# The loads of combine's residual rows, moved behind the last expert's weights

## The reference, cut to what matters

```python
x = x + g1 * (merged @ w_out)
h2 = rms_norm(x) * (1.0 + sc2) + sh2
x = x + g2 * hier_moe(h2, w_rg, b_rg, w_re, b_re, w_gate, w_up, w_down)
```

## Time and profile before

| | |
|---|---|
| median of 3 runs | 1881.39 us (1880.12 to 1888.14) |
| profiled execution, its own time | 1881.47 us |
| its span in the profile | 1879.6 us |
| PE busy | 1624.2 us, 86% of the span |
| DVE busy | 850.9 us, 45% |
| ACT busy | 350.0 us, 19% |
| POOL busy | 222.8 us, 12% |
| moved by DMA | 197.16 MB, mean 105 GB/s |

### The profile page before, as it was taken

How to read it: one execution, slowest core, us unless ns; L and a number is a source line. 1 busy time by engine, 2 the same in 40 slices (tenths; PEclk the granted TensorE clock), 3 DMA queues, 4 the chain that set the end, 5 groups by cost and what they waited for, 6 DMA issues and landing times. The chain is left out here.

```text
span 1879.6 us, 18009 instructions
## 1 busy us (share of the span) xinstructions
PE 1624.2 (86%) x6099; PEld 955.6 (51%) x6100; DVE 850.9 (45%) x1740; ACT 350.0 (19%) x726; POOL 222.8 (12%) x387
## 2 busy tenths in 40 slices
PE   7799968869879799999989999899997299899980
PEld 1455623367734466666646777654554244444440
DVE  1311219855057999999983333332111511111116
ACT  2311110011145111111114444400111011111110
POOL 0000020000031011111110000000322012222220
PEclk9899989967589899999999999899998599999995
DMA  9100035420010311122100300052222846667647
GB/s 341 63 4 4 5 107 186 131 27 3 1 32 12 115 58 58 58 59 78 60 30 0 138 1 1 21 198 74 101 97 78 300 148 216 239 218 274 218 157 285
DMA packets 139193, 197.16 MB, mean 105 GB/s; under 512 B 30741, under 2 KB 106069, under 8 KB 138789
## 3 DMA queue, kind: packets, MB, share of 16 engines
q1 hardware_dynamic: 125714, 156.69, 25.5%
q0 software_dynamic: 8800, 28.52, 4.1%
q10 hardware_dynamic: 4612, 11.05, 1.7%
HBM read 154.94 MB, written 39.17 MB: 103 GB/s over the span
## 5 line engine op out<-in xcount | busy, mean ns | idle before, releaser
L1153 DVE TENSOR_SCALAR_CACHE_REDUCE tk_hits<-sc,tk_cand 128x384 bf16<-128x384 f32 (+6 forms) x217 | 250.5, 1154 | 7.7
L1119 PE MATMUL ps<-hT,gt_w 128*128 128x352 f32 (+1 forms) x768 | 240.6, 472 | 12.8 <-DMA gt_w<-in_w_glu 12.8
L1909 PE MATMUL ps<-ex_wgu,ex_xT 128*128 x416 | 187.0, 603 | 17.8 <-SPq L1824 12.1
L1119 PEld LDWEIGHTS ps<-hT,gt_w 128*128 128x128 f32 x768 | 147.1, 192 | 102.5 <-DMA gt_w<-in_w_glu 13.4
L1909 PEld LDWEIGHTS ps<-ex_wgu,ex_xT 128*128 128x128 f32 x416 | 78.1, 193 | 110.0 <-issue 110.0
L1500 PE MATMUL ps<-hT,mergedT 128*128 128x512 f32 (+1 forms) x288 | 127.6, 602 | 4.7 <-DMA op_wr<-in_w_route_expert 4.7
L1119 PE MATMUL ps<-zT,gt_w 128*128 128x352 f32 (+1 forms) x384 | 120.9, 468 | 0.0
L1331 DVE CUSTOM_DVE_ANT_0 at_s<-ps,mask 128x1024 f32<-128x1024 f32 (+8 forms) x76 | 58.8, 778 | 104.1 <-PE ps L1243 91.4
L1982 DVE SCALAR_TENSOR_TENSOR ex_hid<-ex_silu,ex_weight,ps 128x256 f32<-128x256 f32 x26 | 12.5, 480 | 202.0 <-ACT ex_silu L1954 202.0
L1119 PEld LDWEIGHTS ps<-zT,gt_w 128*128 128x128 f32 x384 | 73.0, 190 | 44.0
L1930 PE MATMUL ps<-ex_wd,ex_hidT 128*128 x208 | 93.6, 592 | 0.2 <-DVE ex_hidT L1989 0.2
(11 more groups left out here) (428 smaller groups left out, 2156.6 us busy)
## 6 DMA issues: line engine op xcount, KB each, us to landing
ex_wgu<-in_w_gate SPq DMA_DIRECT2D x16, 1024.0 KB, 5.9
ex_wgu<-in_w_up SPq DMA_DIRECT2D x16, 1024.0 KB, 11.0
ex_wd<-in_w_down SPq DMA_DIRECT2D x16, 1024.0 KB, 12.9
sp_ada_w<-in_w_ada SPq DMA_DIRECT2D x14, 1024.0 KB
gt_w<-in_w_in SPq DMA_DIRECT2D x16, 512.0 KB, 5.3
cb_y<-y_dram ACTq DMA_DIRECT2D x16, 512.0 KB, 8.3
merge_left_dram<-qiT SPq DMA_DIRECT2D x8, 544.0 KB, 6.3
mg_gb<-gate_b_dram SPq DMA_DIRECT2D x8, 544.0 KB, 3.7
```

What stands on the lines that cost most here:

```text
L1119: i = nc.tensor.matmul(m.ps[:, seq % 8, 0:n], w[:, c % NB, at + k, :], rhs[:, k, lo:lo + n], start=k == 0, stop=k == nk - 1)
L1153: return v.tensor_scalar(hits[0:r, 0:w], m.sc[0:r, c:c + w], scalar, 0.0, ALU.is_ge, ALU.add, accum_out=cnt[0:r, j:j + 1])
L1909: j = nc.tensor.matmul(m.ps[:, 2 + b, :], xT[:, b, k, :], wgu[:, bass.ds(at, 1), k, :].rearrange("p o n -> p (o n)"), start=k == 0, stop=k ...
```

## The change

The loop that issues the nine loads of the residual rows is moved on SP: from between `weights_here(0)` and the loop over the experts 3 to 15 to behind that loop, ahead of the last two calls of `weights_here`. The loads themselves, their places and their semaphore are the same, and so is every other instruction.

```diff
--- before.py
+++ after.py
@@ -1824,13 +1824,13 @@
                     sp.sem_inc(here, 1)
 
                 weights_here(0)
-                for t in range(TILES):
-                    sp.dma_start(m.x1[t][0:rows_of(t), :], m.x1_dram[t * P:t * P + rows_of(t), :]).then_inc(m.x1l, 16)
                 for e in range(RING, NE):
                     weights_here(e - RING + 1)
                     used = sp.value_load(m.expert_done[0:1, e - RING:e - RING + 1], min_val=1, max_val=MAXT)
                     sp.wait_ge(dn, used)
                     load_expert(nc, sp, m, A, e)
+                for t in range(TILES):
+                    sp.dma_start(m.x1[t][0:rows_of(t), :], m.x1_dram[t * P:t * P + rows_of(t), :]).then_inc(m.x1l, 16)
                 for e in range(NE - RING + 1, NE):
                     weights_here(e)
```

## The result

The changed kernel took 1891.35 us (median of 12 runs, 1886.93 to 1899.81) beside 1881.6 us for the kernel before in the same comparison: a ratio of 1.005, 95% interval 1.0033 to 1.0066, which is 9.4 us, between 6.2 and 12.4. A later comparison with runs of its own gave 1890.89 beside 1885.08: 1.0027 (1.0009 to 1.0045), 5.1 us. The change makes the kernel slower by about 0.4%, some 7 us; the forecast was +4.7 us. One run of a kernel further down (the signals first) took 2064.89 us, in a slower state of the chip, and is left out of that kernel's figures. The profiled execution took 1893.06 us, its span 1891.2.

A forecast was written before the change was run, and what follows sets the result against it. PE's matmul tiles bound the expert stage, through waits for first gathers (12.5 us) and SP's weight signals (12.1 us). Terms -4.6 (gathers) + 7.4 (late signal) + 1.9 (clock) = +4.7 on 1881.47 gave 1886.2 us, range 1881.5 to 1891.0.

The forecast's parts named there:

- the rows' transfer was hidden: Before combine: residual rows leave the queue by 1812.7, PE's last matmul ends at 1827.70, so 15 us are left.
- no hold: Rival at SP's late issues: an issue counts as done once its own packets are listed; +1.7 us, 1883.2 us, chance 0.2.
- By bytes: Rival at SP's queue: megabytes, not packets, fill it; signal 14.2 us late, +11.5, 1892.9 us, chance 0.12.
- PE is not held by it: Rival: PE's idle before 1789.39 had another, earlier cause, so only the gain is left; 1876.8 us, chance 0.05.
- the size of the hold: At the nine late issues on SP: the signal comes 7.4 us later than 1789.0, bounds 4.4 to 8.9.
- that gate load: The third expert's gate load on SP, ended with 1598 packets left; taken as the room for the nine issues.
- the one bound: Room of 1331 packets, from the second expert's up load: SP free at 1797.9, signal 8.9 us late.
- The gain: At the first two gathers, with the nine loads gone: second transposes start 4.6 us earlier, bounds 3.4 and 4.9.
- empty-queue price of 4.4 us: Landing time of a gather with SP's queue empty, applied to both first gathers to get the 4.6 us.
- The clock: At PE's late idle: the granted clock falls and costs 1.9 us, bounds 1.7 and 2.0.
- no measurable change: Whole kernel: the forecast lies within half a per cent, 9.4 us; chance of staying within 0.84.
- the range: Whole kernel's predicted time: 1881.5 to 1891.0 us.

The follow-up runs named there:

- the signals first: Against the kernel before, SP signals expert e-1 ahead of issuing expert e's loads: row loads in the new place 1873.97 us (0.9936), in the old place 1877.18 us (0.9952).
- the second profile: The changed kernel unedited, timed and profiled again beside the kernel before: ratio 1.0027 (1.0009 to 1.0045).
- the loads behind the signal: Against the changed kernel, the nine row loads stand behind the signal for expert 14, ahead of expert 15's: 1882.23 us, 0.9996 of the kernel before.
- no loads at all: Against the changed kernel, the nine row loads and combine's wait for them are left out: 1881.29 us, 0.999 of the kernel before.
- the rows loaded twice: Against the changed kernel, all nine row loads are also issued at the old place, combine waiting for eighteen: 1895.19 us, 1.0064 of the kernel before.
- two loads ahead: Against the changed kernel, two of the nine row loads stay ahead of the signal for expert 14, seven go behind it: one run, 1883.6 us.

## Why the prediction went as it did

**The mechanism, step by step, was right.** The gathers gained, the nine issues were held by the last expert's packets, the signal behind them came late, PE waited for it and met the low clock, the rows' transfer was hidden. Of the rivals, *no hold* doesn't agree with the runs: a load of 64 rows held SP for 6.58 us and one of 1024 rows for 0.60. The Trainium skill, page "Perfetto Trace Analysis", section "DMA Instruction — HWDGE (DVE, Sync)", behind that rival, has the sequencer free when its own instruction's descriptors have been generated; these two times differ from it, and the measurement decides. *By bytes* doesn't fit either: when the ninth issue ended, 7.34 - 2.43 = 4.9 MB were outstanding, where 3.15 would have been its limit. *PE is not held by it* falls with the 10.75 us.

**The step that failed is the size of the hold.** "I take 7.4, because eight of the nine stand behind a load of few packets, as that gate load did": the hold came to 8.70 us. The room (the packets of earlier loads still outstanding when an issue ends) was not 1598 packets but 1342 at the ninth issue's end, close to the 1331 that had been taken as the one bound (its 8.9 us hit). The row chosen as nearest ended its issue after 0.71 us, so it may not have been held to its limit at all. The prediction had a nearer one, the row load that the first stage's weights held for 5.72 us, which ended with 1310 left; it was used against *by bytes* alone. But the kernel before had no single room to read: its other three issues that were held long, the second expert's down load and the third's up and down loads, ended at 1467.09, 1471.40 and 1475.55, when this many packets of SP's queue from 1455 were through:

```profile
q1 hardware_dynamic: 3138, 3.67, 91.9%
...
q1 hardware_dynamic: 4617, 5.17, 96.4%
...
q1 hardware_dynamic: 5446, 6.77, 98.1%
```

4720, 6032 and 7072 packets stood ahead of them, so 1582, 1415 and 1626 were left. What sets the room between 1310 and 1626 no run shows.

**The gain was a little over-sized.** 4.6 was forecast, 3.77 measured. The single empty-queue price of 4.4 us held for the first gather (4.5), but the second, issued 1.84 us behind it, took 5.5; the bound of 3.4 us, from a gather of 5.8, was nearer.

**The clock** was sized at 1.9 and cost 2.05 us (1.5 in the second profile, 8.64 - 7.13).

**What can be told from no change** was put at half a per cent. The first comparison's interval reaches 0.17% to either side, so a change of 0.5% is clear of noise there; the forecast's "no measurable change" was too coarse.

Together the measured terms give -3.77 + 8.70 + 2.05 = +7.0 us instead of +4.7. The two comparisons, +9.4 (6.2 to 12.4) and +5.1 (1.7 to 8.5), both contain it, and their mean is 7.2. On the median of before shown at first the terms make 1888.4; the measured median lies 3 us above that, and 0.35 us above the range's upper end of 1891.0. That remainder is not a part of the change that the runs could find: before itself had medians of 1881.6, 1883.78, 1884.27 and 1885.08 us in four comparisons, which is as wide. The second comparison's 1890.89 us lie within the range; on which side of its end a median falls is chance at this size, the 2.3 us between +4.7 and +7.0 are not.

What stays open is how much of the 3.8 us at the first gathers reaches the end. Against before, the loads behind the signal and no loads at all give 0.8 and 1.9 us by their ratios; late against early loads give 3.2 us with the signals first by the medians, and 2.7 or 7.0 with the rows loaded twice by the ratios. All have the same sign, and each is uncertain by some 3 us or more. The gain itself is in every profile: from the end of routing's last matmul group (line 1670) to the first gate/up it is 15.9 to 16.4 us in the four with row loads beside the first gathers and 12.1 to 12.7 in the nine without. But between the first gate/up and expert 14's, those nine have 13 groups of 8.8 us behind waits of about 2 us (none to two each) and the four have 2 (none or one each), at 1.7 us a group. That would take back a part of the gain; whether it is chance or follows from the earlier start is not shown.

## What to carry to other kernels

A DMA issue is not free to the queue that issues it: ask how much is already outstanding there and who waits for the instruction behind it, here a signal that PE needed 0.4 us later. Give a signal ahead of the issues that don't depend on it; doing so throughout the loop won 9 us with the row loads in their old place and 12 with them late, more than the nine loads' whole effect. Where a backlog is unavoidable, put the largest load last and make few of them, since an issue waits for what is ahead of it and not for itself; and read a queue's room from all issues that were plainly held, as a spread and not as one number.

## What the runs showed of the hardware that was not expected

How long an issue on SP's queue takes doesn't go by its own size: 64 rows took 6.58 us behind 1024, and 1024 rows 0.60 us behind 64. The issues that were held late in the last expert's drain ended with 1342 to 1449 packets of earlier loads outstanding. That is not a fixed room: earlier in the drain issues ended sooner, the first row load's with 1824 left and that of the 1024 rows standing last with 2432 - 819 = 1613 (819 packets went through from 1780.5 to 1784.81).

The granted clock fell even though PE was already back at work. With two loads ahead PE resumed at 1788.63 at the full level, after 3.47 us, and lost it from about 1789.3 to 1792.8 (PE's stretches):

```profile
1787.80:1788.80 1.00, 0.17 (x1) 1.00 1.04 331
1788.80:1789.80 1.00, 1.00 (x2) 0.77 1.04 298
1789.80:1790.80 1.00, 1.00 (x3) 0.50 0.91 261
1790.80:1792.80 2.00, 2.00 (x4) 0.51 1.06 411
1792.80:1793.80 1.00, 1.00 (x3) 1.00 1.02 406
```

The group took 8.82 us, about as much as behind a wait of 6.82 us (8.90). Waits of 2 us were followed by such a group in some cases (8.83) and not in others (7.13), so one wait of 2 us costs at times 1.7 us more than itself.
